# Moving three ScalarE copies, three attention transposes and one head's normalisation to other places in their engines' queues

## The reference

```
h   = RMSNorm(x);  z = h @ W_in          # columns: u | v | q | k | values
A   = gelu(u) * (W_s @ LayerNorm(gelu(v)) + b)          # 4 channel groups, 128-row blocks
B   = (softmax(q1 k1') - lam * softmax(q2 k2')) @ values # 4 heads, block-causal
B   = RMSNorm per head of B
x   = x + RMSNorm(concat(A, B) @ W_out)
x   = x + RMSNorm((silu(g) * up) @ W_down),  [g | up] = RMSNorm(x) @ W_gate_up   # 2816 wide
```

## Time and profile before

| | before |
|---|---|
| time, median of 3 runs | 1116.6 us (1113.69 to 1116.83) |
| the profiled execution: its own time | 1115.11 us |
| the profiled execution: span of the trace | 1113.3 us |
| mean granted TensorE clock (share of 2.4 GHz) | 0.997 |
| busy share: TensorE, its weight loads, VectorE, ScalarE, GpSimd | 98%, 87%, 52%, 52%, 52% |
| chain that ended last, by engine | TensorE 87%, VectorE 5%, ScalarE 4% |
| DMA | 118.33 MB, 106 GB/s over the span |

### The profile page before, as it was taken

One profiled execution on the slowest core, in us unless ns is written; L12 is line 12 of the kernel. 1 busy time (PEld: TensorE's weight loads), 2 busy tenths in 40 slices (PEclk: granted clock), 3 DMA queues, 4 the chain that ended last, 5 costly groups with the idle time before them and its releaser, 6 DMA issues.

```text
span 1113.3 us, 17390 instructions
## 1 busy us (share of the span) xinstructions
PE 1093.7 (98%) x6763; PEld 964.3 (87%) x6763; DVE 583.9 (52%) x982; ACT 580.3 (52%) x1129; POOL 577.0 (52%) x454
## 2 busy tenths in 40 slices
PE   9999999999999999999999999999899999999998
PEld 6877777999999999888887777789899999998886
DVE  3353524778888885000254445438788888830103
ACT  5656684565555555222356557746555555532212
POOL 3534254566666665644434324545766666656440
PEclk9999999999999999999999999999999999999999
DMA  8323213413333343622243221224234333353212
GB/s 274 128 62 95 65 50 95 151 43 111 114 114 94 97 115 120 222 98 99 81 130 126 81 68 60 73 75 134 81 110 114 108 94 104 115 193 128 95 57 76
DMA packets 144777, 118.33 MB, mean 106 GB/s; under 512 B 3747, under 2 KB 119989, under 8 KB 144694
## 3 DMA queue, kind: packets, MB, share of 16 engines
q1 hardware_dynamic: 144692, 117.20, 33.6%
q10 hardware_dynamic: 2, 0.00, 0.0%
HBM read 110.90 MB, written 6.29 MB: 105 GB/s over the span
## 4 chain that ended last, share of the span: by engine, by line
PE 87%; DVE 5%; ACT 4%; POOL 1%; issue 1%; DMA 1%; SPq 0%; DVEq 0%; ACTq 0%; POOLq 0%
PE banks L583 27%; PE banks L585 27%; PE banks L584 27%; PE banks L642 2%; PE banks L672 1%; DVE o_rows L1532 1%; PE banks L592 1%; PE banks L657 1%; ACT swap L1153 1%; DMA raw<-in_w_in_dram 1%; PE banks L686 1%; POOL w_lo L508 0%; DVE s_part L1643 0%; DVE banks L1636 0%; POOL w_lo L526 0%
## 5 line engine op out<-in xcount | busy, mean ns | idle before, releaser
L508 POOL TENSOR_TENSOR w_lo<-raw,w_hi 128x512 fp32r<-128x512 f32 x204 | 259.6, 1297 | 312.6 <-ACT w_hi L1026 312.6
L526 POOL TENSOR_TENSOR w_lo<-raw,w_hi 128x512 fp32r<-128x512 f32 x200 | 258.1, 1299 | 142.8 <-ACT w_hi L1088 137.9
L583 PE MATMUL banks<-xg_hi,w_hi 128*128 128x256 f32 (+1 forms) x896 | 279.2, 312 | 5.6 <-ACT m L1320 5.6
L585 PE MATMUL banks<-xg_lo,w_hi 128*128 128x256 f32 (+1 forms) x896 | 275.4, 307 | 0.0
L584 PE MATMUL banks<-xg_hi,w_lo 128*128 128x256 f32 (+1 forms) x896 | 275.1, 307 | 0.0
L1026 ACT ACTIVATE w_hi<-raw 128x1024 fp32r<-128x1024 f32 x102 | 107.1, 1056 | 172.1 <-PE banks L585 156.5
L1088 ACT ACTIVATE w_hi<-raw 128x512 fp32r<-128x512 f32 x200 | 125.7, 631 | 126.9 <-DVE raw L1669 65.2
L583 PEld LDWEIGHTS banks<-xg_hi,w_hi 128*128 128x128 f32 x896 | 172.1, 192 | 13.8 <-ACT m L1320 6.2
L585 PEld LDWEIGHTS banks<-xg_lo,w_hi 128*128 128x128 f32 x896 | 172.0, 192 | 8.0
L584 PEld LDWEIGHTS banks<-xg_hi,w_lo 128*128 128x128 f32 x896 | 172.2, 192 | 6.5
L583 PE MATMUL banks<-w_hi,hid_hi 128*128 128x512 f32 x352 | 137.4, 390 | 0.0
(11 more groups left out here) (160 smaller groups left out, 1796.8 us busy)
## 6 DMA issues: line engine op xcount, KB each, us to landing
raw<-in_w_gate_up_dram SPq DMA_DIRECT2D x88, 512.0 KB, 4.1
raw<-in_w_down_dram SPq DMA_DIRECT2D x44, 512.0 KB, 3.5
raw<-in_w_in_dram SPq DMA_DIRECT2D x40, 512.0 KB, 3.7
raw<-in_w_out_dram SPq DMA_DIRECT2D x16, 512.0 KB, 3.5
x_spill<-x_rows SPq DMA_DIRECT2D x8, 512.0 KB, 5.0
x_rows<-x_spill SPq DMA_DIRECT2D x8, 512.0 KB, 5.4
x_rows<-in_x_dram SPq DMA_DIRECT2D x4, 512.0 KB, 7.5
out_dram<-x_rows SPq DMA_DIRECT2D x8, 256.0 KB, 2.0
```

The lines of the kernel that those rows point to most:

```text
L508: last = tt(lo[:, piece], raw_half(l, c, h)[:, piece], hi[:, piece].bitcast(F32), ALU.subtract)
L526: tt(lo, full, hi.bitcast(F32), ALU.subtract).then_inc(w_ready, 1)
L583: mm(o, stat[0], mov[0], start=first, stop=False)
L585: return mm(o, stat[0], mov[1], start=False, stop=last)
```

## The change

Only calls move; no instruction is added or removed. It has four parts, in each of the two layers:

- TensorE: `turn(8)`, `turn(9)`, `turn(10)` (the last with `weigh(4)`) each go behind the half of the u projection that followed them. On ScalarE, `copy_turned(9)`, `copy_turned(10)` and `take_heads(4)` each go behind the `exponentials` call that followed.
- ScalarE: the roots of heads 0 to 2 go ahead of `gated_high(3)` and of the weight rounding `high(l, 11, 1)`; `head_high(0)` goes ahead of `high(l, 12, 0)`.
- VectorE: `head_low(0)` goes ahead of the reciprocal and scaling of head 3.
- ScalarE: the copy of the first product. For f = F0 it goes from a place behind five other calls (`hidden_high(1)`, two `s_high`, two `factor_high`) to just ahead of them; for every later f it goes from behind `silu_21(f - 1)` to ahead of it.

```diff
@@ block.tensor @@
                 qk_half(l, 7, upper)
+                u_half(l, 0, lower)
                 turn(l, 8)
-                u_half(l, 0, lower)
                 scores(l, 10)
+                u_half(l, 0, upper)
                 turn(l, 9)
-                u_half(l, 0, upper)
                 scores(l, 11)
+                u_half(l, 1, lower)
                 turn(l, 10)
                 weigh(l, 4)
-                u_half(l, 1, lower)
                 scores(l, 12)
@@ block.scalar @@
                 copy_turned(8)
+                exponentials(10)
                 copy_turned(9)
-                exponentials(10)
                 copy_u(0)
                 high(l, 10, 0)
+                exponentials(11)
                 copy_turned(10)
-                exponentials(11)
+                exponentials(12)
                 take_heads(4)
-                exponentials(12)
                 copy_u(1)
...
                 gated_high(2)
+                head_roots(0, 0, H - 1)
                 gated_high(3)
                 high(l, 11, 1)
-                head_roots(0, 0, H - 1)
                 take_heads(7)
                 head_roots(1, H - 1, H)
+                head_high(0)
                 high(l, 12, 0)
-                for h in range(H - 1):
-                    head_high(h)
+                head_high(1)
+                head_high(2)
                 high(l, 12, 1)
-                head_high(H - 1)
+                head_high(3)
...
                 factor_high(l, F0, T2)
+                copy_m1(F0)
                 hidden_high(1)
...
                     if f > F0:
                         silu_11(f - 1)
+                        copy_m1(f)
                         silu_21(f - 1)
-                    copy_m1(f)
@@ block.vector @@
                     scale_head(h)
+                head_low(0)
                 head_rs(1, H - 1, H)
                 scale_head(H - 1)
-                for h in range(H):
+                for h in range(1, H):
                     head_low(h)
```

## The result

The changed kernel takes 1104.6 us in the median of 4 runs (1104.20 to 1106.95); the kernel before, with one more run on the same chip, takes 1115.9 us (1113.69 to 1116.83). The ratio is 0.991, with a 95% interval from 0.990 to 0.993: 8 to 11 us faster. The profiled execution of the changed kernel took 1104.67 us, with a span of 1102.9 us.

A forecast was written before the change was run, and what follows sets the result against it. TensorE, busy 98% of the span, bounds the kernel. Gains of 7.1 us (turns, heads), 1.8 and 2.4 (copies, second and first layer) sum to 11.3: 1115.1 becomes 1103.8, or 1105 as median; range 1101.5 to 1110.

The forecast's parts named there:

- Turns: TensorE's stop ahead of turn(8): moving the turns removes the full 1.19 us per layer, with no new wait.
- Heads: TensorE's waits at turn_head(0) and out_k(4): earlier roots, scales and head_low(0) remove 1.12 and 1.23 us per layer.
- The copy at F0: First product's copy at tile F0: it fills a ScalarE hole and removes TensorE's 2.54 us wait.
- The new wait at F0 + 1: Following tile's copy, behind silu_11(F0): TensorE newly waits 1.87 us there, in both layers.
- Later copies: The 38 later copies passing silu_21: cost 0, with 0.4 us of cover.
- That rival: Copies ahead of silu_21 make all 38 passes late, at 0.6 us each: 1128 us; chance 0.03.
- The first layer's clock: TensorE's half clock behind the first layer's wait at F0 goes with that wait, gaining 1.7 us.
- The rival of that name: Clock falls behind the new 1.87 us wait, costing 1.7 us in one layer (1106.7) or both (1108.4); chance 0.14.

The follow-up runs named there:

- e1: Kernel before with only the turns moved on TensorE, and ScalarE's three calls for them: 1112.84 us, ratio 0.9981.
- e2: Kernel before with only the roots, head_high(0) and head_low(0) moved: 1110.16 us, ratio 0.9960.
- e6: Kernel before with only the roots of heads 0 to 2 moved, head_high(0) and head_low(0) left in place: 1115.09 us, ratio 1.0008.
- e4: Kernel before with only the later copies moved ahead of silu_21, tile F0's copy left in place: 1113.85 us, ratio 0.9984.
- groups A to C: Three sets of follow-up runs, each sharing a chip with runs of the kernel before, which took 1114.47, 1114.27 and 1114.76 us.
- e5: Kernel before with both moves of the copy, tile F0's and the later ones, and nothing else: 1111.9 us, ratio 0.9978.
- e7: Changed kernel with 16 filler matmuls of ones on TensorE ahead of the second copy's wait: 1106.35 us, ratio 0.9928 to before.
- e9: Changed kernel with 8 filler matmuls of ones on TensorE ahead of the second copy's wait: 1104.84 us, ratio 0.9908 to before.
- e3: Kernel before with only the copy of tile F0 moved, later copies still behind silu_21: 1119.65 us, ratio 1.0039.

## Why the prediction was right, step by step

- **Turns, 1.19 us a layer.** As predicted; `exponentials(10)` starts where it did (130.28, and 0.95 for the earlier start, is 131.23 against 131.22), and nothing waits for it or for the copies behind it. e1 shows it alone.
- **Heads, 1.12 and 1.23 us a layer.** As predicted, e2 shows it. But the reason given was too narrow. The fourth scale was to end 0.3 us ahead of TensorE; it starts at 165.4 and lasts 1.33, so it ends at 166.7 to TensorE's 166.77: next to no margin. And the text gave "Heads 1 and 2 end near 170.4 and 171.2" without saying why GpSimd would leave VectorE alone there. It does so only because of the moved `head_high(0)`; e6, without that move, gains nothing.
- **The copy at F0, 2.54 us a layer.** As predicted: in the second layer it starts at 775.56 when B11 is done, and `hidden_high(1)`, at 776.35, still waits only for VectorE.
- **The new wait at F0 + 1, 1.87 us.** 788.81 - 786.76 - 0.12 = 1.93, in both layers, behind `silu_11` as described.
- **Later copies, 0.** e4 shows it, which was not slower and had no later wait. That rival is out.
- **The first layer's clock, 1.7 us.** This term failed in the profile: the sum took full clock behind the new wait. The clock fell there, so the 1.7 us were kept. The rival of that name is what happened in the profiled execution. With it the sum is 11.3 - 1.7 = 9.6 us, and the ruler shows 9.4. The four runs have mean clocks of 0.998 three times and 0.997 once (that one took 1106.95), so probably it fell in each too; only one of them was profiled, so this is read from means alone.

So why was 1105.0 hit to 0.5 us with a term of 1.7 us wrong? By the prediction's own price one fall gives 1106.7. But the profile after began 1.0 us sooner, and the forecast had been lifted by 1.5 us to the median of three runs of before, which later runs put lower (medians of 1114.3 to 1114.8 in groups A to C). These two made up for it: 1.5 + 1.0 - 1.7 = 0.8 us too high. The waits and their sizes were right, the clock behind the new wait was not, and that its 1.7 us did not show in the time was luck.

## What to carry to other kernels

When a copy or a rounding that TensorE waits for is moved, ask what stands ahead of it now and what *that* waits for: moving only the first of a series moved the wait one tile on and made it longer. Two calls that look like one edit may work on different engines: `head_high(0)` mattered through the hole that it opened in GpSimd's queue. And when a few microseconds matter, subtract what lies ahead of the first edit, and count clock falls, before comparing two profiles.

## What the runs showed of the hardware

- **The same idle stretch does not always lower the clock.** Behind idles of 2.38 to 2.40 us it fell in five of ten places profiled (first layer of before, e2 and e6, both layers of e1; not in the second layer of before, e2 and e6, nor in e4), behind 1.77 us in two of four (first layer of after, second of e5), behind 0.77 to 0.85 us in none of five, behind 3.5 us in both, and for longer. What decides it no run here shows. e4's runs, of one kernel, split into levels about 2.4 us apart, mostly with the mean clock; a single fall is 1.7, and one run of the slower level has a mean clock of 1.000, so something else parts the levels too, and it stays open. The Trainium skill, "TensorE: Matmul & The Clock Gate", section "What's actually happening", has the watch run freely, and different outcomes of equal idles agree with that. With the wait filled by matmuls (e7, e9) it did not fall in any of four places.
- **A fall costs more behind a longer idle:** 1.7 us behind 1.77 or 2.38 us, 2.8 us behind 3.5 (e3, both layers).
- **The start varies.** TensorE's first `scores` began between 53.85 and 56.77 us in twelve profiles, with nothing changed ahead of them. Only one execution of each kernel was profiled, so it is not shown how much of the spread of one kernel's runs this is; the runs of before in group A spread over 3.6 us (1113.66 to 1117.21).
